# Prompt attention of layer 1: quads of four heads in eight phases, v as the stationary operand, masks added by matmuls

## The reference

```python
p_cmp = masked_softmax(ein('bqhgd,bnhd->bqhgn', q, kc) * scale, mc)          # 63 compressed keys
o_cmp = ein('bqhgn,bnhd->bqhgd', p_cmp, vc)
o_sel = ein('bqhgk,bqhkd->bqhgd', masked_softmax(ein('bqhgd,bqhkd->bqhgk', q_rot, ks) * scale, ms), vs)
mw = ((kw_pos[None, :] >= 0) & (dlt >= 0) & (dlt < WIN_C))[None, :, None, None, :]
o_win = ein('bqhgn,bnhd->bqhgd', masked_softmax(ein('bqhgd,bnhd->bqhgn', q_rot, kw) * scale, mw), vw)
o = gates[..., 0:1] * o_cmp + gates[..., 1:2] * o_sel + gates[..., 2:3] * o_win
```

## Time and profile before

| what | us |
|---|---|
| median of 3 runs | 5569.19 |
| profiled execution, device time | 5574.27 |
| its span, first to last instruction | 5571.9 |
| PE busy in the span | 4083.8 (73%) |
| DVE busy | 1780.2 (32%) |
| ACT busy | 1027.4 (18%) |
| POOL busy | 1418.1 (25%) |
| the stage, from its first DMA to the next stage's first | 3326.9 to 4321.0 |

### The profile page before, as it was taken

How to read it: one execution, slowest core, us unless ns; L and a number is a source line. 1 busy time by engine, 2 the same in 40 slices (tenths; PEclk the granted TensorE clock), 3 DMA queues, 4 the chain that set the end, 5 groups by cost and what they waited for, 6 DMA issues and landing times. The chain is left out here.

```text
span 5571.9 us, 71854 instructions
## 1 busy us (share of the span) xinstructions
PE 4083.8 (73%) x24308; PEld 3762.5 (68%) x24308; DVE 1780.2 (32%) x4191; ACT 1027.4 (18%) x2254; POOL 1418.1 (25%) x992
## 2 busy tenths in 40 slices
PE   5998054445507999996925657888888458799998
PEld 4997043345406999995825656777777237799998
DVE  1001322143352222222031115556666232222224
ACT  2000033301121111111001113334444110111111
POOL 4332300010004444444230002222111002644441
PEclk7999555555658999998966765579999678899999
DMA  3222511241151111111872121100000321111111
GB/s 124 85 91 75 184 53 53 82 191 35 61 170 36 57 45 45 45 38 39 284 240 61 60 54 27 25 22 22 20 20 17 100 83 39 53 45 45 45 45 46
DMA packets 358869, 398.91 MB, mean 72 GB/s; under 512 B 114760, under 2 KB 316008, under 8 KB 355756
## 3 DMA queue, kind: packets, MB, share of 16 engines
q1 hardware_dynamic: 311936, 266.55, 15.5%
q10 hardware_dynamic: 33260, 78.31, 4.4%
q0 software_dynamic: 13552, 52.52, 2.8%
HBM read 331.39 MB, written 134.15 MB: 84 GB/s over the span
## 5 line engine op out<-in xcount | busy, mean ns | idle before, releaser
L486 PE MATMUL ffn_hid_psH<-ffn_x_hi,ffn_hid_w_hi 128*128 128x352 f32 x2112 | 683.3, 324 | 59.7 <-POOLq L441 59.7
L488 PE MATMUL ffn_hid_psH<-ffn_x_hi,ffn_hid_w_lo 128*128 128x352 f32 x2112 | 680.0, 322 | 0.0
L487 PE MATMUL ffn_hid_psH<-ffn_x_lo,ffn_hid_w_hi 128*128 128x352 f32 x2112 | 679.4, 322 | 0.0
L486 PEld LDWEIGHTS ffn_hid_psH<-ffn_x_hi,ffn_hid_w_hi 128*128 128x128 f32 x2112 | 397.5, 188 | 60.6 <-issue 60.6
L487 PEld LDWEIGHTS ffn_hid_psH<-ffn_x_lo,ffn_hid_w_hi 128*128 128x128 f32 x2112 | 398.8, 189 | 0.0
L488 PEld LDWEIGHTS ffn_hid_psH<-ffn_x_hi,ffn_hid_w_lo 128*128 128x128 f32 x2112 | 397.9, 188 | 0.0
L2004 PE MATMUL nsa_p_psO<-nsa_p_vrow,nsa_p_pT 128*128 128x64 f32 x2112 | 334.5, 307 | 42.4 <-ACTq L1911 35.6
L2004 PEld LDWEIGHTS nsa_p_psO<-nsa_p_vrow,nsa_p_pT 128*128 128x128 f32 x2112 | 301.3, 218 | 92.9 <-ACTq L1911 75.0
L545 DVE TENSOR_TENSOR hT<-ffn_hid_psD,hT 128x352 f32<-128x352 f32 x528 | 276.9, 525 | 230.0 <-PE ffn_hid_psD L505 230.0
L504 PE MATMUL ffn_hid_psD<-ffn_hid_h_lo,ffn_hid_d_hi 128*128 128x352 f32 x1056 | 340.6, 323 | 0.0
L505 PE MATMUL ffn_hid_psD<-ffn_hid_h_hi,ffn_hid_d_lo 128*128 128x352 f32 x1056 | 340.6, 323 | 0.0
(11 more groups left out here) (508 smaller groups left out, 8372.1 us busy)
## 6 DMA issues: line engine op xcount, KB each, us to landing
out<-in_cache_a_kv ACTq DMA_DIRECT2D x8, 4088.0 KB
ffn_hid_raw<-in_w_ffn_gate SPq DMA_DIRECT2D x44, 512.0 KB, 4.5
ffn_hid_raw<-in_w_ffn_up SPq DMA_DIRECT2D x44, 512.0 KB, 5.7
ffn_hid_raw<-in_w_ffn_down SPq DMA_DIRECT2D x44, 512.0 KB, 3.7
z_ab<-ab_in_o SPq DMA_DIRECT2D x90, 218.0 KB, 2.0
ab_in_raw<-in_w_in_ab POOLq DMA_DIRECT2D x20, 872.0 KB, 5.2
dil_s_kv<-in_cache_a_kv SPq DMA_DIRECT2D x16, 1024.0 KB, 31.0
cmp_pg<-in_cache_c_cmp_kv SPq DMA_DIRECT2D x128, 128.0 KB, 2.0
```

Source lines behind the costliest of these rows:

```text
L486: nc.tensor.matmul(psH[:, g, m, 0:N], hi, x_hi[:, k, cols(g)], start=(k == 0), stop=False)
L487: nc.tensor.matmul(psH[:, g, m, 0:N], hi, x_lo[:, k, cols(g)], start=False, stop=False)
L488: last = nc.tensor.matmul(psH[:, g, m, 0:N], lo, x_hi[:, k, cols(g)], start=False, stop=(k == KD - 1))
```

## The change

Only `nsa_prompt` changes. A quad of four heads that share keys is now the unit: 4 quads per tile, 32 in all. A quad has 8 phases, an even one for the selected branch of a head and the odd one after it for its window and compressed branches. Three quads are in work at a time: in the phases of quad u, PE scores quad u, turns and multiplies the weights of quad u-1, and turns back the sums of quad u-2. The selected scores have the banks `psS` and the others `psW`, so phase n waits for the exponentials of phase n-2 (before, a head waited for the head ahead of it). There are no runs and no loops; the whole list is unrolled.

- Products with v: v (128x64) is the stationary operand, and the turned weights of four heads (512 columns) are the moving one. The selected sum is written to PSUM partitions 0 to 63 and the window's to 64 to 127 of the same bank (`psO`), the compressed one to 64 to 127 of another (`psC`). The sums are then transposed, so they are copied out (`oT`, `cmpT`) and turned back on PE (8 turns per quad).
- Turned weights: one step turns one block of the selected branch (ACT copies its 512 columns) and one of the window or the compressed branch (DVE copies). Queries, keys and sums that are turned use the same two banks `psR`.
- Masks: added on PE by products of an identity with the mask, inside the accumulation of the scores. DVE no longer adds masks.
- Queries: loaded four heads at a time, split on POOL before they are turned, and copied by ACT and DVE. Keys: turned tile by tile, one tile ahead, instead of all before the first unit.
- Scaling and adding: ACT scales the compressed sum, DVE the other two, POOL adds. The result goes out once per tile.

Core of the diff (the lines removed are in the listing above):

```diff
+    def steps(u):
+        i = tile_of(u)
+        sel = [(0, a, a * P, P) for a in range(i + 1)]
+        rest = [(1, a, SELW + (a - low(i)) * P, P) for a in range(low(i), i + 1)] + [(2, 0, CM, NCMP_P)]
+        return list(itertools.zip_longest(sel, rest))
+    def part(u, p):
+        n = len(steps(u))
+        return range((p - 1) * n // (PH - 1), p * n // (PH - 1)) if p else range(0)
...
+                def score(u, p):
+                    i, kv, h, br = tile_of(u), kv_of(u), p // 2, p % 2
...
+                    if PH * u + p >= 2:
+                        pe.wait_ge(exp_done, PH * u + p - 1)
...
+                        M(ps[:, c:c + n], q(0), kT[:, 0, br * KVH + kv, k], start=True, stop=False)
+                        if br == 1 and i >= WT and c == 0:
+                            M(ps[:, 0:P], one[:], edge[:], start=False, stop=False)
+                        if c + n == width:
+                            M(ps[:, width - P:width], one[:], diag[:], start=False, stop=False)
+                        last = M(ps[:, c:c + n], q(0), kT[:, 1, br * KVH + kv, k], start=False, stop=True)
...
+                def turn(u, s):
+                    for slot, piece in enumerate(steps(u)[s]):
...
+                        claim(slot, "p", u, s)
+                        pe.wait_ge(exp_done, PH * (u + 1) - (0 if br else 1))
+                        for h in range(HQ):
+                            last = T(psR[0:n, slot, h * P:(h + 1) * P], p_[:, u % 2, h, col:col + n], ident)
+                        last.then_inc(turned[slot], 1)
+                def product(u, s):
...
+                        pe.wait_ge(evicted[slot], slot_use(slot, "p", u, s) + 1)
...
+                        ps = (psO[0:DC], psO[DC:P], psC[DC:P])[br]
+                        last = M(ps, v, pT[0:n, order[u, s] % 2, slot], start=first, stop=end)
+                    last.then_inc(used, 1)
...
+                for u in range(QUADS + 2):
+                    for p in range(PH):
+                        if u < QUADS:
+                            score(u, p)
+                        if p == 0 and u >= 2:
+                            product(u - 2, len(steps(u - 2)) - 1)
+                        if p == 2 and u + 1 < QUADS:
+                            if (u + 1) % 4 == 0:
+                                turn_keys(tile_of(u + 1))
+                            turn_queries(u + 1)
+                        if p == 3 and u >= 2:
+                            turn_back(u - 2)
+                        if 1 <= u <= QUADS:
+                            for s in part(u - 1, p):
+                                turn(u - 1, s)
+                                if s:
+                                    product(u - 1, s - 1)
```

More of the change, by code:

```diff
@@ L1872, in nsa_prompt @@
[L1872 to L1911, removed]
+        halves = sb("halves", [P, 2, 2, HQ, 2, DC])
@@ L1923, in _ @@
[L1923 to L1933, removed]
+                        sp.dma_start(krow[:, j, :, twice], qk[r, CQ:CQ + 2 * KVW].rearrange("t (b d) -> t b d", d=DC)).then_inc(keys_loaded[j], 16)
@@ L1937, in _ @@
                 T, M = nc.tensor.transpose, nc.tensor.matmul
[L1938 to L1948, removed]
@@ L2018, in _, with evict_piece @@
+            def evict_piece(eng, copy, slot, u, s):
+                piece = steps(u)[s][slot]
+                if piece is None:
+                    return
+                n, at = piece[3], order[u, s]
+                eng.wait_ge(turned[slot], slot_use(slot, "p", u, s) + 1)
+                if at >= 2:
+                    eng.wait_ge(used, at - 1)
+                copy(pT[0:n, at % 2, slot], psR[0:n, slot]).then_inc(evicted[slot], 1)
             @block.scalar
@@ new lines, in read_sums, with back @@
+                def read_sums(u):
+                    act.wait_ge(used, order[u, len(steps(u)) - 1] + 1)
+                    if u:
+                        act.wait_ge(turned[1], slot_use(1, "back", u - 1) + 1)
+                    copy(oT[:], psO[:]).then_inc(o_read, 1)
+                def back(u):
+                    act.wait_ge(turned[0], slot_use(0, "back", u) + 1)
+                    act.wait_ge(w_ready, u + 1)
+                    if u >= 2:
+                        act.wait_ge(merged, u - 1)
+                    for h in range(HQ):
+                        last = a.activation(m2[:, u % 2, h], psR[:, 0, h * DC:(h + 1) * DC], ACT.Copy, scale=w[:, u % 2, h, 2:3])
+                    last.then_inc(evicted[0], 1)
@@ new lines, in _ @@
+                queries(0)
+                for u in range(QUADS + 2):
+                    for p in range(PH):
+                        n = PH * u + p - 1
+                        if 0 <= n < PH * QUADS:
+                            exponentials(n // PH, n % PH)
+                        if p == 1 and u >= 2:
+                            read_sums(u - 2)
+                        if p == 2 and u + 1 < QUADS:
+                            queries(u + 1)
+                        if p == 3 and u >= 2:
+                            back(u - 2)
+                        if 1 <= u <= QUADS:
+                            for s in part(u - 1, p):
+                                evict_piece(act, copy, 0, u - 1, s)
@@ new lines, in _ @@
+                v.tensor_copy(diag[:], causal)
+                v.tensor_copy(edge[:], early)
+                v.tensor_copy(cT[:, 0], KP)
+                v.drain()
+                v.tensor_copy(ends[:, :, 0:NCMP_P], cmask)
+                v.tensor_tensor(cT[:, 1], KP, cT[:, 0].bitcast(F32), ALU.subtract)
+                v.drain().then_inc(masks_ready, 1)
+                keys(0)
+                queries(0)
+                for u in range(QUADS + 2):
+                    for p in range(PH):
+                        if u < QUADS:
+                            maxima(u, p)
+                        if p == 1 and u >= 2:
+                            read_compressed(u - 2)
+                        if p == 1 and 1 <= u <= QUADS:
+                            weights(u - 1)
+                        if p == 2 and u + 1 < QUADS:
+                            if (u + 1) % 4 == 0:
+                                keys(tile_of(u + 1))
+                            queries(u + 1)
+                        if p == 3 and u >= 2:
+                            back(u - 2)
+                        if 1 <= u <= QUADS:
+                            for s in part(u - 1, p):
+                                evict_piece(dve, v.tensor_copy, 1, u - 1, s)
```

413 lines of the change are left out of this document (232 added, 181 removed).

## The result

The changed kernel took 5381.05 us, the median of 4 runs (5369.11 to 5390.5), against 5569.93 for the kernel before on the same chip; the ratio is 0.9661, 95% interval 0.9633 to 0.9688. Forecast were 5356, so the direction and nearly all of the size held, and the end was 25 us later. The stage runs from 3327.70 to 4139.56, the next stage's first DMA: 812 us against 994, where 781 were forecast. The profiled execution took 5390.5 us (span 5388.9), the longest of the four.

A forecast was written before the change was run, and what follows sets the result against it. PE was taken as the bound. Work 658, waits 48 and 22, ends 23 and clock 30 made a stage of 781 us against 994, 213 less, so 5356 us for the kernel; range 5255 to 5470.

The forecast's parts named there:

- 658 of work at the full clock: PE's work in tiles 0 to 7: scores 203, weight turns 130, queries and sums 61, products 196, switches 68 us.
- 70 of waits: PE waiting for late copies in phases 2 and 3 of tiles 2 to 7, 48 us; short phases in tiles 0 and 1, 22.
- 23 of ends: Stage's ends: preparation some 8 us, first quad's scores alone 5, last quad's weights and sums alone 10.
- 30 of clock: Half clock in tile 0 and half of tile 1 costs 30 us; the clock was expected to rise in tile 1.
- Products with v: 592 PE instructions of 512 moving columns, put at 196 us between ends of 126 and 253, against 277 before.
- 3T: PE time for a step's products in both halves; T is one 512-column instruction, 0.427 us; one piece alone takes 2T.
- Switches: PE pauses of 0.15 us at each change between 128-wide and 64-wide work; 68 us in all, ends 0 and 77.
- three-engine rival: Waits by design between three engines; bites only in early tiles, within Rival 1's range, without a chance of its own.
- DVE's relief gives PE nothing back: Claim that the mask additions DVE loses gave PE nothing back by themselves; the masks cost PE 45 us.
- Rival 2: PE gets away cheaper: T per product (70 us less) or no switching cost (68 less); about 5285 us, chance 0.13.
- rival 3: Clock rises as late as before, half clock through tiles 1, 2 and part of 3; 5450 us, chance 0.10.
- Rival 1: Halves don't help (2T per product, 57 us more) or phase 2 and 3 waits double (48 more); about 5410, chance 0.20.

The follow-up runs named there:

- e5: Against the changed kernel: ten unneeded 512-column products put into PE's wait for keys, at seven places; 5367.47 us, ratio to before 0.9630.
- e3: Against the changed kernel: key turns moved to phase 5; turns of queries, sums and keys, and their copies, put behind a phase's steps; 5338.11 us.
- e4: Against the changed kernel: mask products leave PE, and DVE adds the masks in PSUM ahead of its maxima again; 5402.03 us.
- e1: Against the changed kernel: window sum moved to partitions 0 to 63 of another bank, so a step's two products use the same array half; 5479.24 us.

## Why the prediction came out as it did

The forecast of the stage was 658 of work at the full clock, 70 of waits, 23 of ends and 30 of clock. Two terms were mis-sized, in opposite directions.

- **Products with v: 196 forecast, about 150 by the measured steps.** The prediction chose 3T for a step with both halves, though the trace it had could tell: in a narrower view of the earlier trace rows two instructions start together at 4564.28 and the next two at 4564.44, so they run two at a time from the start, and not only the second of one half beside the first of the other. Measured is 2T for 120 steps, 4T for the 12 where the compressed piece stands beside a selected one, 2T for 32 pieces alone: 352 x 0.427 = 150. The Trainium skill (TensorEngine Tiling (Array Packing), "Key Properties") has tiles that work in parallel, which the prediction gave as 56 us less; the trace agrees for full pieces, and the 63-row piece takes 10 of the 56 back.
- **Switches: near.** Eight turns ahead of the products take 0.96 from start to start (4012.99 to 4013.95) for 0.88, a pair has 0.15 beyond its 2T, and the first score behind 0.11 more than the others: 0.34 for the two changes of a step, where 0.30 was put. Scores, turns and the copies off PE were near too: DVE at 53% and ACT at 49% fell just short of the 55 to 70% given, and the last long stretch, four quads in 130 us, lies just above the 29 to 32 each.
- **Waits: 70 forecast, 81 measured** (100.3 idle less 9.3 and 9.6 at the two ends, forecast 23). The sum is near, its parts were not: the wait for keys, 21.5 us, was not seen. The prediction counted the four key turns on PE, and DVE's 0.35 per quad as work that is hidden. It did not ask what stands on DVE ahead of those copies: the sums' copy, the weights and a maximum. "No pause above 2 us on PE" failed there. The three-engine rival did not come.
- **Clock: 30 forecast, about 92 estimated from the profile.** This step failed. With two levels, a mean of 0.87 is 26% of 812 us at 1.2 GHz, 211 us; taking PE as busy in 88% of that, as in the whole stage, gives 185 us, and half of that is lost. "Above 0.9 from tile 2 on" was 0.83 and 0.84 in two stretches. The prediction let the clock rise once and stay, since the change "leaves no such pause" as the 5.55 us; the trace shows it fall again in every tile from tile 1 on, behind waits of phases 2 and 3 like the 1.53 and 0.74 us above. e5 shows the cause at the wait for keys, e3 that shorter queues behind the turns bring 1.00. The Trainium skill (TensorE: Matmul & The Clock Gate, "A second HAM failure mode: psum-queue depth-cycling") tells of a kernel where "the PE micro-idles between MM groups frequently enough that HAM oscillates" (HAM is its name for what grants the clock); here the like is seen with PSUM banks that wait for a copy, 0.84 in the stretch of 110 us.
- **Masks: the sentence that DVE's relief gives PE nothing back was wrong.** e4 has 38 us more idle time on PE without it.

Together: 612 (658 less the 46 us of the products) + 81 + 19 + 92 = 804, against 812 measured. So the forecast came near by luck: 46 us too much for products stood against some 62 too few for the clock. Rival 2 was nearer for the products (126) and rival 3 for the clock (127); each by itself was further off in the time. Rival 1's half without overlap is what e1 made: 5479 where the rival said 5410, mainly since its 57 us were counted from 3T, not from 2T.

Where the stage's 182 us came from reads differently by the same estimate of the clock. Of the 829 us that PE was busy before, at a mean clock of 0.78, some 182 were lost at 1.2 GHz; now it is some 92 of 712. So about 90 us of the gain are clock, 64 are idle time (165 to 100), and only some 28 are less work at the full clock (647 to 619). The 88 us of e1 and the 11 to 15 of e4 are what the new form would lose without these parts, not shares of that sum. That idle time and clock gained from the run ends, the preparation and the third quad in work is argued, not shown: none of these was undone alone.

## What to carry to other kernels

Two 64-column products into the two partition halves of one bank ran side by side, so a 64-wide stationary operand is worth pairing with another of the same height; look in the trace whether each pair does overlap, since the 63-row piece in another bank did not. Where the bound engine's bank must be copied by another engine, list what stands ahead of that copy on its queue, and put the request behind work that does not need the answer. Price a pause on TensorE as the pause plus what the work behind it loses at 1.2 GHz; where it can't be removed, filling it with products nobody reads may pay.

## What the runs showed of the hardware

- A pair of plain fp32 products, 64 stationary columns and 512 moving ones each, takes 1.01 us with its switch in the two halves of one bank and 1.87 in the same half of two banks. A 63-row product behind a 128-row one, in the other half and another bank, did not overlap: 1.00 each.
- Instructions that compute nothing needed saved time in e5: 14 to 20 us by the medians, 17 to 21 us of the stage, with 70 of them.
- The granted clock rose inside tile 0 once PE had 64 fillers there: 1.00 from 3360 to 3380. Without them it was 0.50 from 3360 to 3370, with PE recorded busy for 9.13 of 10 us.
